# Cross attention beside the query projections, and expert routing computed from unnormalised rows

## What is computed

```python
h = rmsnorm(x, norm_xattn)
q = (h @ wq).reshape(s, 4, 512); k, v = mem_n @ wk, mem_n @ wv      # 4 heads of 512
p = softmax(q @ k.T * 512 ** -0.5)                                  # head by head, 256 x 256
x = x + concat(p @ v) @ wo

h = rmsnorm(x, norm_ffn)                                            # 1/rms per row, a gain per feature
p_group = softmax(h @ router_group)                                 # 4 groups, the best one is taken
sel = (h @ router_expert)[the 4 experts of that group]              # the best 2 are taken
y = sum over the chosen experts: combine * (silu(h @ w_gate[e]) * (h @ w_up[e])) @ w_down[e]   # 16 experts, 2048 -> 512 -> 2048
out = rmsnorm(x + y, norm_final)
```

## Time and profile before

| | us |
|---|---|
| median of 3 runs | 3093.89 (3092.44 to 3095.89) |
| the profiled execution | 3096.74 |
| its span (first to last instruction) | 3095.3 |
| PE busy in the span | 2863.4 (93%) |
| DVE, ACT, POOL busy | 1467.1, 1209.4, 22.3 |
| DMA queue of SP (weights) | 610.31 MB of 686.26 MB |

### The profile page before, as it was taken

How to read it: one execution, slowest core, us unless ns; L and a number is a source line. 1 busy time by engine, 2 the same in 40 slices (tenths; PEclk the granted TensorE clock), 3 DMA queues, 4 the chain that set the end, 5 groups by cost and what they waited for, 6 DMA issues and landing times.

```text
span 3095.3 us, 34900 instructions
## 1 busy us (share of the span) xinstructions
PE 2863.4 (93%) x13080; PEld 2151.9 (70%) x13080; DVE 1467.1 (47%) x1696; ACT 1209.4 (39%) x1517; POOL 22.3 (1%) x24
## 2 busy tenths in 40 slices
PE   6999998999999999999999899999999987888896
PEld 5887877777877888888887788788777664333332
DVE  4444544555655555555555744667553552111122
ACT  4443544553344444444444544544443342101111
POOL 0000000000000000000000000000000001000000
PEclk9999999999999999999999999999999998999999
DMA  7665654446644554555554565544445455999997
GB/s 264 237 216 195 246 194 171 167 162 217 229 167 168 184 188 178 190 178 188 183 183 163 202 248 190 204 163 170 177 169 191 153 189 230 392 419 393 420 401 294
DMA packets 121243, 686.26 MB, mean 222 GB/s; under 512 B 12413, under 2 KB 17965, under 8 KB 45872
## 3 DMA queue, kind: packets, MB, share of 16 engines
q1 hardware_dynamic: 83808, 610.31, 52.8%
q10 hardware_dynamic: 35040, 62.42, 5.7%
q0 software_dynamic: 2288, 12.08, 1.2%
HBM read 655.89 MB, written 33.59 MB: 223 GB/s over the span
## 4 chain that ended last, share of the span: by engine, by line
PE 80%; DMA 11%; DVE 4%; ACT 2%; issue 2%; DVEq 1%; ACTq 1%; SPq 0%; PEldq 0%; PEld 0%
PE PS L287 21%; PE PS L289 21%; PE PS L288 21%; PE PS L1798 6%; DMA WIDE<-in_w_up 4%; DMA WIDE<-in_w_down 2%; DMA WIDE<-in_w_gate 2%; PE PS L317 2%; PE PS L1749 1%; PE PS L1332 1%; DVE LO L243 1%; DMA WORK<-proj 1%; DMA WORK<-xkv 1%; PE PS L1872 1%; PE PS L865 0%
## 5 line engine op out<-in xcount | busy, mean ns | idle before, releaser
L243 DVE TENSOR_TENSOR LO<-RAW,HI 128x1024 fp32r<-128x1024 f32 x776 | 941.0, 1223 | 906.8 <-ACT HI L241 902.5
L287 PE MATMUL PS<-HI,XH 128*128 128x512 f32 (+1 forms) x3104 | 1241.0, 400 | 22.8 <-DVE XL L326 9.9
L289 PE MATMUL PS<-HI,XL 128*128 128x512 f32 (+1 forms) x3104 | 1226.7, 395 | 0.0
L288 PE MATMUL PS<-LO,XH 128*128 128x512 f32 (+1 forms) x3104 | 1225.7, 395 | 0.0
L241 ACT ACTIVATE HI<-RAW 128x1024 fp32r<-128x1024 f32 x776 | 812.9, 1057 | 914.9 <-PE PS L289 803.6
L287 PEld LDWEIGHTS PS<-HI,XH 128*128 128x128 f32 (+1 forms) x3104 | 582.7, 188 | 165.5 <-issue 11.2
L288 PEld LDWEIGHTS PS<-LO,XH 128*128 128x128 f32 (+1 forms) x3104 | 582.3, 188 | 137.2 <-issue 1.0
L289 PEld LDWEIGHTS PS<-HI,XL 128*128 128x128 f32 (+1 forms) x3104 | 581.5, 187 | 137.5
L1798 PE MATMUL PS<-WIDE,XS 128*64 128x512 f32 x1024 | 233.1, 600 | 42.1 <-DMA WIDE<-in_w_up 29.7
L1798 PEld LDWEIGHTS PS<-WIDE,XS 128*64 128x64 f32 x1024 | 77.7, 137 | 183.4 <-issue 183.2
L485 DVE TENSOR_TENSOR X<-PS,X 128x1024 f32<-128x1024 f32 x88 | 107.7, 1224 | 48.1 <-PE PS L289 45.3
(11 more groups left out here) (309 smaller groups left out, 1417.6 us busy)
## 6 DMA issues: line engine op xcount, KB each, us to landing
RAW<-in_w_in SPq DMA_DIRECT2D x132, 1024.0 KB, 4.8
RAW<-in_w_mlp_in SPq DMA_DIRECT2D x64, 1024.0 KB, 4.8
RAW<-in_w_mlp_out SPq DMA_DIRECT2D x64, 1024.0 KB, 4.8
WIDE<-in_w_gate SPq DMA_DIRECT2D x64, 1024.0 KB, 11.9
WIDE<-in_w_up SPq DMA_DIRECT2D x64, 1024.0 KB, 13.7
WIDE<-in_w_down SPq DMA_DIRECT2D x64, 1024.0 KB, 14.1
RAW<-in_w_out SPq DMA_DIRECT2D x32, 1024.0 KB, 4.8
RAW<-in_xattn_wkv SPq DMA_DIRECT2D x32, 1024.0 KB, 4.8
```

What stands on the lines that cost most here:

```text
L243: dve.tensor_tensor(r["lo"][:, hl, :], r["raw"][:, k, :], r["hi"][:, hl, :].bitcast(F32), ALU.subtract).then_inc(lo_done, 1)
L287: pe.matmul(o, xh, wh, start=kt == 0, stop=False)
L288: pe.matmul(o, xh, wl, start=False, stop=False)
L289: mm = pe.matmul(o, xl, wh, start=False, stop=kt == kn - 1)
```

## The change

It has three parts.

1. **Cross attention head by head.** A query unit is no longer stored: `query` copies it to SBUF (`MQ`), and that head's attention is put into the hooks of the next query unit, behind its blocks 2, 3, 5 and 6; its output is transposed behind block 0 of the unit after. The fourth head's attention is in the hooks of the first `add_head`. The loop is written out. Keys and values have two buffers: `kv_load` of the first two heads stands ahead of the query units, on ACT's queue, that of heads 2 and 3 behind `result` of two heads before. Finer semaphores (`m_kqT`, `m_qT`, ...) take the place of PE's drain (L1453) and of shared counters.
2. **Routing from raw rows.** The router's weights take the gain (`router_weights`, behind block 2 of the third `add_head`). In the last `add_head` X is transposed and split unnormalised: `rows_T_of_x(c)` behind block 2c+2 and `router_part(c)` (12 products) behind block 2c+3, for the first three chunks of 512 columns; the fourth follows the stage. `tokens(c)` has ACT copy a chunk of X to the high token rows and POOL write the low ones. The row factor 1/rms is applied to the 20 logits. The choice is made on 16 columns at once, in 21 DVE operations, and one slot product goes. The tables' loads move to the second query unit, the load of the gain row goes.
3. **The norm at the gather's eviction.** Each gather starts with two fp32 products (`RR`, each row's factor, by the 0/1 matrix) which give the factor of every gathered slot; ACT copies them to `RB`. Each of the four steps is evicted by four DVE operations of 128 x 256, which multiply with the gain and `RB`. The first gather is interleaved with the first pair's gate products: gather step 0 and 1, product 0, step 2, product 1, step 3, product 2, product 3. `weights()` follows its last step.

```diff
+        def kv_load(u):
+            if u >= 2:
+                act.wait_ge(m_kqT.h, u - 1)
+                act.wait_ge(m_value.h, u - 1)
+            for dst, c in ((MK[u % 2], 0), (MV[u % 2], D)):
+                m_kv[u % 2].inc(act.dma_start(dst, cols_of(XKV, u * 512 + c)), 16)
+        for u in range(2):
+            kv_load(u)
...
+            def query(pair, ready):
+                act.wait_ge(pe_done, ready)
+                act.wait_ge(m_kqT.h, u)
+                state["query"] = ev[pair].h, ev[pair].inc(act.activation(MQ..., pair_ap(pair)..., ACT.Copy))
...
-            return loads, {1: transposes, 2: scores, 3: softmax, 4: probs_T, 5: values}, result
+            return query, {2: transposes, 3: scores, 5: probs_T, 6: values}, result
...
+        def rows_T_of_x(c):
+            pe.wait_ge(*x_final[c])
+            x_T[c] = transpose_split(X, 4 * c + 4, 16, banks=(4, 5), j0=4 * c)
+        def tokens(c):
+            t = slice(c * 512, (c + 1) * 512)
+            act.wait_ge(*x_final[c])
+            pool.wait_ge(m_thi.h, m_thi.inc(act.activation(HTOK[0][:, :, t], X[:, :, t], ACT.Copy)))
+            m_tlo.inc(pool.tensor_tensor(HTOK[1][:, :, t], X[:, :, t], HTOK[0][:, :, t].bitcast(F32), ALU.subtract))
...
-        for u in range(4):
-            extra = dict(first) if u == 0 else {}
-            result = None
-            if u == 3:
-                loads, hooks, result = cross(0)
-                extra = dict(hooks={0: loads, **{k + 1: f for k, f in hooks.items()}})
+        for u in range(heads):
+            query, hooks, following = cross(u)
             s = Stage()
-            store(u % 2, s.gemm(8, 0, u % 2, **extra), u % 2, cols_of(XQ, u * 512))
+            query(u % 2, s.gemm(8, 0, u % 2, **extra))
             s.end()
-        result()
-        with loop(3, {...}) as it:
-            ...
+            extra = dict(hooks={**hooks, **({0: result} if result else {})})
+            result = following
+        add_head(0, extra["hooks"])
+        add_head(1, {0: result})
+        add_head(2, {2: router_weights})
+        for c in range(3):
+            parts[2 * c + 2] = lambda c=c: rows_T_of_x(c)
+            parts[2 * c + 3] = lambda c=c: router_part(c)
+        add_head(3, parts, finish_chunk)
+        rows_T_of_x(3)
+        mm = router_part(3)
...
-                act.wait_ge(m_gath.h, m_gath.inc(mm))
-                m_slots.inc(act.activation(XS[:, 4 * u:4 * u + 4, :]..., PS[:, bank:bank + 2, :]..., ACT.Copy))
+            dve.wait_ge(m_gath.h, m_gath.inc(mm))
+            for k in range(4):
+                ins = dve.scalar_tensor_tensor(out=XS[:, 4 * u + k, :], in0=PS[...], scalar=GAIN[:, 5, 4 * u + k:4 * u + k + 1], in1=RB, op0=ALU.mult, op1=ALU.mult)
+            m_slots.inc(ins)
```

More of the change, by code:

```diff
@@ L1431, in build @@
         XD = float(W512) ** -0.5
-        small_load([a["router_group_2"][0], a["router_expert_2"][0]], 20)
[L1435 to L1442, removed]
+        heads = D // W512
+        m_kv = [Count(ctx, nc, f"m_kv{b}", 0) for b in range(2)]
@@ L1534, in build @@
-        s.end()
-        state["hidden"] = s_lo.now()
-        router = small_split(20)
-        s = Stage()
-        add_head(s, after=column_sums)
-        s.end()
-        bank_free[:] = [s_lo.now()] * 4
-        fence()
+            if u == 1:
+                routing_tables()
+            extra = dict(hooks={**hooks, **({0: result} if result else {})})
[3 more added lines that the diff above has]
+        add_head(2, {2: router_weights})
@@ L1546, in build @@
+        for h in range(NH):
+            mm = pe.transpose(PS[:, 7, h * 20:(h + 1) * 20], LOGT[:, h * P:(h + 1) * P], IDENT[0:20, 0:20])
+        logits_T = T(mm)
+        column_sums(3, squares=SQUARES)
+        factors_of_x()
+        tokens(3)
+        bank_free[:] = [s_lo.now()] * 4
+        for e in (act, dve, pe):
+            for x in (s_act, s_dve, s_pe):
+                e.wait_ge(x.h, x.now())
+        all_stored()
         work_memory.close()
         WIDE = sb("WIDE", [P, WIDE_SLOTS, BLK])
-        WORK = sb("WORK_MOE", [P, 2432])
@@ L1838, in expert_pair @@
                 pick(g + 1)
-                gather(g + 1)
+                for u in range(4):
+                    gather(g + 1, u)
             pe.wait_ge(m_hid.h, m_hid.now())
@@ L1880, in build @@
             pick(0)
-            dve.wait_ge(s_act.h, htok_hi)
-            token = []
-            for r in range(8):
-                token_lo(r)
-                token.append(s_dve.now())
-            gather(0, token)
-            weights()
-            combined = s_dve.now()
             for p in range(N_EXP // 2):
@@ L1942, in build @@
                     split(experts + b)
+                for e in (act, dve):
+                    e.wait_ge(m_tlo.h, m_tlo.now())
+                lead, hooks, ready = first_unit(GAIN[:, 5, :], 16, scaled=(X, R1ST))
+                lead()
+                for j in range(4):
+                    hooks[j]()
+                pe.wait_ge(s_lo.h, ready[7])
                 weights()
@@ L2010, in make_plan @@
         plan.append((1, unit("xattn_wq_2", u)))
-    plan.append((3, rows("xattn_wo_2", 0, 4)))
-    plan.append((1, rows("xattn_wo_2", 3, 4)))
+    for u in range(4):
+        plan.append((1, rows("xattn_wo_2", u, 4)))
     for passes, first in ((N_EXP // 2 - 1, 0), (1, N_EXP // 2 - 1)):
```

346 lines of the change are left out of this document (195 added, 151 removed).

## The result

The changed kernel takes **3069.7 us** (median of 4 runs, 3066.3 to 3071.6) against 3093.2 (4 runs, 3092.3 to 3095.9); the ratio is 0.992, with an interval of 0.9904 to 0.9939. That is 2.8 us under the forecast of 3072.5, inside its range of 3062 to 3082. Its profiled execution took 3071.6 us, with a span of 3070.0 (before: 3095.3).

What follows compares the result with a forecast made beforehand. PE bounds the dense products and the weights' stream the experts. Terms of -8.4 (cross attention, last `add_head`), -18.8 (chain to the first release) and +5.8 (stream) sum to -21.4 us: 3093.9 becomes 3072.5 us, range 3062 to 3082.

Steps and rivals of the forecast that it cites:

- The bound: Whole kernel: PE bounds the dense products; the weights' stream bounds the experts, where PE's spare time counts for nothing.
- Part 1: Cross attention: removes 18.2 us of waits and 3.2 of half clock, adds 1.9 for `kv_load`.
- the 18.2: Cross attention: PE's waits of 9.1 us for keys and values, 8.2 at a head's end, 0.9 of issue; all removed.
- Part 2a: Last `add_head`: transposes and router products add 6.9 us of work, waits of two chunks add 4.2.
- The upper bound for the waits: Last `add_head`: POOL holds DVE's LO, so PE waits 2.0 us on XL; 2.1 taken for each of two chunks.
- Part 2b: Last cross-attention product to the first `in_w_up` issue: 51.8 us become 33.0, -18.8 us.
- The forecast without a hold: Whole kernel: if POOL did not hold DVE, the sum would be about -26 us instead of -21.4.
- Part 3: Experts' stream: 3 x 1.6 = +4.8 us at the later gathers, 1.0 at the second and third release; +5.8 us.
- The interleave: First gather's steps between the first pair's products: 0.0 to 1.7 us of idle at the second and third release, 1.0 taken.
- the rival on the clock: Last `add_head` to first release: clock falls to 1.2 GHz and stays; up to +34 us, 3106 at worst; chance 0.03.
- waits came back in new places: Cross attention: half of the 18.2 us stays, some 2 us a head, 9 us; 3081 us; chance 0.14.
- the chain was not shorter: Judged rival: no hold by POOL (2.35 us), shorter waits per chunk (2.2), router products at full clock; 3066 us; chance 0.20.
- eaten in the stream: Experts: PE bounds them after all, so the gain ahead of the first release is lost later; about 3085 us; chance 0.03.

Runs made afterwards that it cites:

- a3: The kernel before with only the head-by-head cross attention of the changed kernel; routing, chain and gathers as before; median 3071.4 us.
- b6: The changed kernel with row factor behind the experts' first products, POOL's subtractions in DVE's idle stretches, and first keys and values loaded inside the first query unit; 3054.3 us.
- a1: The changed kernel run again without any edit, as the measure for the other runs; median 3068.0 us.
- a2: The changed kernel with POOL's four low-token-row subtractions started only when the choice of experts is finished; median 3068.8 us.
- b5: The changed kernel with POOL's subtractions where DVE is idle: three behind DVE's addition of the next chunk, the fourth behind the first 0/1 matrices; median 3065.3 us.
- b3: The changed kernel with the row factor applied after the experts' first products, the gain at the eviction split over ACT and DVE; median 3058.2 us.
- a4: The changed kernel without the experts' row norm and gain (left out of the computation), each gather step evicted by one ACT copy; median 3057.9 us.

## Why the prediction was right, point by point

**The bound** was read rightly. The weights' stream is what PE must release, and PE's spare time in it absorbed nothing of what was saved ahead of R: in a3 E came 23.5 us earlier, counted from S, and the end 24.1, with 503.6 us from R on instead of 503.8.

**Part 1.** "I take nothing left of the 18.2" held: no wait on keys, values or the head's end is left. The half clock behind the gaps went as summed (3.2). What the sum lacked is the 2.4 us that stops cost beside their waits, and the 0.5 of half clock at the first products. `kv_load` was put at +1.9 and cost 0.9, since its four issues (2285.75 to 2287.68) lie partly beside ACT's squares of X; b6 got these 0.9 back.

**Part 2a.** The work was put at 6.9 and the waits at 4.2; a3 against a1 gives 9.3 together, of it 3.4 of waits (2.12 and 1.31 us), so 5.9 of work. The router's products were mis-sized: 12 took 1.4 us at full clock and not 1.8, a figure that I had taken from 48 products that ran partly at half clock. The upper bound for the waits (2.1) was right for the first chunk, too high for the second, and the reason given holds: a2 and b5 took POOL away and left 0.8.

**Part 2b** was forecast within 0.6 us. Its marks after E came at 2.4, 7.4, 17.3, 20.6 and 28.9 us where the sum has 2.9, 8.0, 17.9, 21.4 and 29.4. Inside the last step two errors cancel: the two factor products (L1801) took 2.08 us, at half clock, where the sum has 0.9, and the two gather steps 4.33 where it has 5.3. POOL's hold of DVE in the choice, 2.35 by one row of 0.18 us, was 2.0.

By the rule of the Trainium skill (page "SBUF — State Buffer", section "SBUF: two separate sides") the loser of the lock is blocked for the whole instruction. The traces agree (1.22 to 2.58 us, 0.17 to 2.16, `RR` 0.48 to 3.67). The forecast without a hold, about -26, would have been wrong in its working though near in its number (-25.0 from S).

**Part 3** is the step that failed. "The three later gathers ... +0.7" for the eviction and 0.9 for the products, 1.6 each, is right to 0.1 (17.7 against 16.2). The interleave was put at 1.0 and cost about 1.3. But the stream lost 8.6 and not 5.8, as two more phases at half clock fell into the gathers, 1.6 us each. The first two stretches grew from 17.7 to 19.4 and 19.3 us, as forecast; the excess lies in the third, 16.2 before with no phase in it and 21.0 after with two. The sum took the clock in the gathers as unchanged. I had it only in the rival on the clock, as a stay at half clock from the last `add_head` to R. In the last `add_head` the clock stayed full; it fell at 2533.65, just ahead of the choice, and was at half for 17 us in which PE was busy only 4.95. The kernel before had 23.9 us at half clock between E and R.

```profile
2533.70:2550.70 17.00, 4.95 (x18) 4.52 (x19) 9.21 (x43) 2.02 (x3) 2.34 (x1) 0.50 0.32 135
```

The errors have opposite signs: S to E 5.8 better, the stream 2.8 worse, the chain 0.6 better. That the total was nearer than its parts is luck.

**The rivals.** No waits came back in new places; the hold was there (2.0 us in the choice, 3.4 us of waits), so the chain was not shorter for want of it; the clock did not stay low through the last `add_head`; and what was saved ahead of R was not eaten in the stream (a3).

**What stays open** is when a half-clock phase comes. PE's two longest pauses in a later gather are the wait for the 0/1 matrix, 2.1 or 2.2 us in all ten traces, and the wait for the last eviction: 1.0 us in b3 and b6, 1.2 in before, a3 and a4, 1.8 in the other five. Behind the first pause there was a phase in 18 of the 30 gathers (in these three groups 2 of 6, 6 of 9 and 10 of 15), behind the second in 0 of 6, 1 of 9 and 8 of 15. The second count goes with the length of the pause, but no run changed the pause alone, and the same kernel's traces differ: the first gather of the changed kernel has its phase behind the second pause in one trace and behind the first in the other.

## What to carry to other kernels

Where a stream of weights sets the end, divide the span at the releases: a microsecond saved or spent ahead of the first one, or in a stretch where the stream stands still, counts in full; PE's spare time beside the running stream was worth nothing here. Move POOL's operations on SBUF like work of DVE: put them where DVE is idle, since behind the next mark they only hold up what stands there. A factor per row that is multiplied in on the critical path can often wait until it is a scalar of an operation that runs anyway.

## What the runs showed of the hardware

- POOL's 128x1024 subtraction (2.34 to 2.40 us) holds single DVE instructions with two SBUF inputs (128x8: 2.16 us instead of 0.17), and a fp32 `tensor_scalar` with one (128x32: 2.38 us instead of 0.18). It did not hold XL, which has one input from PSUM (1.29 us for two either way). The hold is on record as a long instruction, not as a wait.
- At the later gathers the clock was at half for 3.4 us each time (27 phases in the ten traces) and then back at full; each began 0 to 2.3 us behind the end of one of PE's two long pauses. Windows of the changed kernel's third gather: the pause (PE 0.31 us busy of 2), then the fall, which comes when PE is fully busy again.

```profile
2912.00:2914.00 2.00, 0.31 (x3) 0.34 (x4) 1.54 (x4) 0.00 (x0) 0.00 (x0) 1.00 0.76 307
2916.00:2920.00 4.00, 4.00 (x14) 1.16 (x12) 0.00 (x0) 0.00 (x0) 0.00 (x0) 0.58 0.00 0
```

- A stop of PE cost about 0.2 us beside the wait that the profile names for it (2.4 us for eleven stops; 0.7 for three in one pass at full clock).
